# Block 1's recurrence: the sequential part of a chunk and the masked products of the next placed between the products of the levels

## What is computed

```python
def _rwkv7_time_mix(z, ...):
    ...
    def step(state, inp):
        r_t, d_t, k_t, v_t, kk_t, b_t = inp
        s_a = jnp.einsum('bhvk,bhk->bhv', state, -kk_t)
        state = state * d_t[:, :, None, :] + s_a[..., None] * b_t[:, :, None, :] + v_t[..., None] * k_t[:, :, None, :]
        return state, jnp.einsum('bhvk,bhk->bhv', state, r_t)
    ...
    _, y = lax.scan(step, jnp.zeros((B, H, N, N), f32), xs)
    ...group norm over each head, bonus, gate
```

## Time and profile before

| | us |
|---|---|
| median of 3 runs | 3438.39 (3433.8 to 3445.05) |
| the profiled execution's own time | 3441.6 |
| its span | 3439.8 |
| mean granted clock over the span | 0.93 |
| PE busy | 3057.2 (89%) |
| DVE busy | 1426.8 (41%) |
| ACT busy | 1173.5 (34%) |
| POOL busy | 1203.9 (35%) |

### The profile page before, as it was taken

One profiled execution on the slowest core, in us unless ns is written; L12 is line 12 of the kernel. 1 busy time (PEld: TensorE's weight loads), 2 busy tenths in 40 slices (PEclk: granted clock), 3 DMA queues, 4 the chain that ended last, 5 costly groups with the idle time before them and its releaser, 6 DMA issues.

```text
span 3439.8 us, 40156 instructions
## 1 busy us (share of the span) xinstructions
PE 3057.2 (89%) x15600; PEld 2375.6 (69%) x15600; DVE 1426.8 (41%) x2055; ACT 1173.5 (34%) x1681; POOL 1203.9 (35%) x558
## 2 busy tenths in 40 slices
PE   7989766778999999798999999978768787899998
PEld 5856535766888886576788887746557566688886
DVE  3017535325521274403356443251377352556442
ACT  3243241224322243543442224333433522542222
POOL 3413421103444444332645443403103221445442
PEclk9989877879999999899999999979889889999999
DMA  3312110004233332223532222302102111532222
GB/s 123 98 61 71 50 34 1 2 2 153 92 98 98 93 134 75 92 80 119 167 100 98 92 98 92 110 22 79 46 28 74 55 53 38 193 112 93 98 93 85
DMA packets 80667, 284.07 MB, mean 83 GB/s; under 512 B 8968, under 2 KB 9096, under 8 KB 79744
## 3 DMA queue, kind: packets, MB, share of 16 engines
q1 hardware_dynamic: 66240, 236.36, 21.3%
q10 hardware_dynamic: 13296, 41.97, 3.3%
q0 software_dynamic: 976, 3.56, 0.3%
HBM read 260.86 MB, written 20.99 MB: 82 GB/s over the span
## 4 chain that ended last, share of the span: by engine, by line
PE 55%; issue 19%; DVE 11%; POOL 9%; ACT 5%; DMA 1%; POOLq 0%; SPq 0%; ACTq 0%; DVEq 0%
PE bank L317 14%; PE bank L319 14%; PE bank L318 14%; POOL slab_r L2558 8%; PE bank L530 2%; PE bank L508 1%; PE bank L424 1%; PE bank L580 1%; DVE work L2355 1%; DVE work L2040 1%; DVE small L2038 1%; PE bank L434 1%; PE bank L759 1%; PE bank L818 0%; DVE work L2027 0%
## 5 line engine op out<-in xcount | busy, mean ns | idle before, releaser
L2558 POOL TENSOR_TENSOR slab_r<-slab,slab_high 128x1024 fp32r<-128x1024 f32 x442 | 1094.4, 2478 | 1764.5 <-ACT slab_high L1031 1764.1
L317 PE MATMUL bank<-xh,slab_high 128*128 128x512 f32 x2256 | 908.2, 403 | 35.6 <-POOL slab_r L2558 31.1
L319 PE MATMUL bank<-xh,slab_r 128*128 128x512 f32 x2256 | 889.8, 394 | 0.0
L318 PE MATMUL bank<-x_raw_r,slab_high 128*128 128x512 f32 x2064 | 815.8, 395 | 0.0
L1031 ACT CAST slab_high<-slab 128x1024 fp32r<-128x1024 f32 x442 | 462.3, 1047 | 450.8 <-DMA slab<-in_w_down 215.3
L318 PE MATMUL bank<-work_r,slab_high 128*128 128x512 f32 x1376 | 547.0, 398 | 0.0
L317 PEld LDWEIGHTS bank<-xh,slab_high 128*128 128x128 f32 x2256 | 431.5, 191 | 148.6 <-POOL slab_r L2558 34.9
L317 PE MATMUL bank<-work_r,slab_high 128*128 128x512 f32 x1184 | 474.0, 400 | 48.6 <-DVE work_r L1782 24.9
L319 PEld LDWEIGHTS bank<-xh,slab_r 128*128 128x128 f32 x2256 | 430.8, 191 | 93.8
L319 PE MATMUL bank<-work_r,slab_r 128*128 128x512 f32 x1184 | 475.5, 402 | 0.0
L318 PEld LDWEIGHTS bank<-x_raw_r,slab_high 128*128 128x128 f32 x2064 | 395.5, 192 | 80.6 <-issue 1.7
(11 more groups left out here) (434 smaller groups left out, 2942.3 us busy)
## 6 DMA issues: line engine op xcount, KB each, us to landing
slab<-in_w_down SPq DMA_DIRECT2D x88, 512.0 KB, 3.3
slab<-in_w_up SPq DMA_DIRECT2D x64, 512.0 KB, 3.2
slab<-in_w_gates SPq DMA_DIRECT2D x56, 512.0 KB, 3.4
slab<-in_w_merge SPq DMA_DIRECT2D x48, 512.0 KB, 3.7
slab<-in_w_gu SPq DMA_DIRECT2D x44, 512.0 KB, 3.5
slab<-in_w_in_a SPq DMA_DIRECT2D x32, 512.0 KB, 3.6
gates<-staging ACTq DMA_DIRECT2D x56, 256.0 KB, 2.2
slab<-in_w_out SPq DMA_DIRECT2D x24, 512.0 KB, 3.3
```

The lines of the kernel that those rows point to most:

```text
L317: first = pe.matmul(bank[b][:, :], wh, mh, start=start, stop=False)
L318: pe.matmul(bank[b][:, :], wh, ml, start=False, stop=False)
L319: end = pe.matmul(bank[b][:, :], wl, mh, start=False, stop=stop)
L2558: pool.tensor_tensor(slab_low[:, slot, :], slab[:, slot, :], plain(slab_high[:, slot, :]), ALU.subtract).then_inc(S("slab_split"), 1)
```

## The change

The recurrence of chunk n and the inverse of chunk n+1 are interleaved in the lists of PE, ACT and DVE.

- PE's `merge_levels` takes a function `beside(lv)` that is called between the first and the second product of each level. For chunks 1 to 3 it issues the preceding chunk's right side in level 1, the inverse times the right side in level 2, the outputs in level 3 and the new state in level 4. For chunks 0 to 2 it issues the next chunk's masked products, heads 0 to 2 in level 4, 3 to 5 in level 5, 6 and 7 in level 6. In level 6 it also issues the chunk's own transposes. Only chunk 0's masked products, and chunk 3's right side, inverse product and outputs, stand alone.
- The pieces set beside the levels use banks 0 to 3 (the masked products all four, where they used two) and have semaphores of their own (`act_beside`, `dve_beside`). The start matrix is turned into banks 6 and 7 instead of 4 and 5.
- Two chunks are alive at once, so masked products, whole inverse, the two level matrices and the packed blocks have two sets of tiles. The second set lies in the memory of `xh` and of `x_raw`, which hold nothing needed at that time (tile numbers from `NW` on).
- DVE masks the heads in levels 4 to 6 behind the level's update, and starts the next inverse behind level 6. ACT copies the transposed tiles behind level 6, then packs the next chunk's blocks, then copies the diagonal blocks of the whole inverse.
- In block 3 the helpers are called in their new, divided form.

The diff, cut to its core:

```diff
+        PRODUCTS, WHOLE, LEVEL_X, PACKED = (40, NW + DC), (50, NW), (48, NW + 2), (53, NW + 4)
+        HEADS_IN = {4: (0, 1, 2), 5: (3, 4, 5), 6: (6, 7)}
...
+            def turn_start(x, first):
...
+            def merge_levels(x, tt, am, off, waits, beside):
...
                         products.append(last[4 + hf])
-                    early_gates(fill)
+                    beside(lv)
                     for hf in halves:
                         pe.wait_ge(*products[hf])
...
+            def whole_inverse(waits, fresh):
...
+            def masked_products(ch, heads):
-                for src, b in ((8, 4), (12, 5), (24, 6)):
-                    tokens = turn([(W(src + c)[:, cs], c * P) for c in range(4)], b, "act")
-                for h in range(8):
+                for h in heads:
+                    r, b = half[h % 2], h % 4
                     if last[b]:
...
+                        .then_inc(psum_for["dve_beside"], hand(b, "dve_beside"))
+                if 7 in heads:
+                    mark(f"products{ch}")
+            def turn_operands(ch):
+                cs = slice(ch * P, (ch + 1) * P)
+                turned_at[ch] = [turn([(W(src + c)[:, cs], c * P) for c in range(4)], b, "act_beside")
+                                 for src, b in ((8, 0), (12, 1), (24, 2))]
+            def right_side(ch):
...
                 if ch:
                     pe.wait_ge(S("state_ready"), n.next(S("state_ready")))
+                for w in turned_at[ch]:
+                    pe.wait_ge(*w)
                 for par in range(2):
-                    if last[4 + par]:
-                        pe.wait_ge(*last[4 + par])
-                at = lambda c, par: bank[4 + par][:, c * HD:(c + 1) * HD]
+                    if last[par]:
+                        pe.wait_ge(*last[par])
...
+                    ins = pe.matmul(at(c, par), W(PRODUCTS[ch % 2] + h)[:, 2 * P:3 * P], W(30)[:, h * HD:(h + 1) * HD],
                                     start=(ch == 0 and c == 0), stop=(c == 3))
                     if c == 3:
-                        ins.then_inc(psum_for["dve"], hand(4 + par, "dve"))
-                early_gates(IN_SEQUENCE)
+                        ins.then_inc(psum_for["dve_beside"], hand(par, "dve_beside"))
+            def inverse_times(ch):
+                whole_inverse(inverse_at[ch], ch < 2)
                 for par in range(2):
-                    pe.wait_ge(*last[4 + par])
-                if last[6]:
-                    pe.wait_ge(*last[6])
+                    pe.wait_ge(*last[par])
+                if last[2]:
+                    pe.wait_ge(*last[2])
...
+                    ins = pe.matmul(bank[2][:, hs], W(WHOLE[ch % 2], 2)[:, h * P:(h + 1) * P], W(57)[:, hs],
                                     start=True, stop=True)
+                ins.then_inc(psum_for["act_beside"], hand(2, "act_beside"))
+            def outputs(ch):
+                at = lambda c, par: bank[par][half[par], c * P:(c + 1) * P]
+                pe.wait_ge(*last[2])
...
+                        ins.then_inc(psum_for["act_beside"], hand(par, "act_beside"))
+            def state(ch):
+                if last[3]:
+                    pe.wait_ge(*last[3])
+                for keys, values in ((28, 56), (29, 30)):
+                    for c, par in pairs:
+                        ins = pe.matmul(bank[3][half[par], c * HD:(c + 1) * HD], W(keys)[:, cols(c, par)],
+                                        W(values)[:, cols(c, par)], start=(keys == 28 and c == 0),
+                                        stop=(keys == 29 and c == 3))
+                ins.then_inc(psum_for["dve_beside"], hand(3, "dve_beside"))
+            masked_products(0, range(8))
+            start_at = turn_start(LEVEL_X[0], 6)
+            for ch in range(NT):
+                def beside(lv, ch=ch):
+                    if ch and lv <= 4:
+                        (right_side, inverse_times, outputs, state)[lv - 1](ch - 1)
+                    if ch < NT - 1 and lv in HEADS_IN:
+                        masked_products(ch + 1, HEADS_IN[lv])
+                    if lv == 6:
+                        turn_operands(ch)
+                inverse_at[ch] = merge_levels(LEVEL_X[ch % 2], 52, lambda lv: 54 + lv % 2,
+                                              lambda h, ch=ch: W(PRODUCTS[ch % 2] + h)[0:HD, HD:P], start_at, beside)
                 if ch < NT - 1:
-                    if last[7]:
-                        pe.wait_ge(*last[7])
-                    for keys, values in ((28, 56), (29, 30)):
-                        for c, par in pairs:
-                            ins = pe.matmul(bank[7][half[par], c * HD:(c + 1) * HD], W(keys)[:, cols(c, par)],
-                                            W(values)[:, cols(c, par)], start=(keys == 28 and c == 0),
-                                            stop=(keys == 29 and c == 3))
-                    ins.then_inc(psum_for["dve"], hand(7, "dve"))
-            pe.wait_ge(*y_token)
+                    start_at = turn_start(LEVEL_X[(ch + 1) % 2], 6)
+            for step in (right_side, inverse_times, outputs):
+                step(NT - 1)
+            y_tokens = [last[0], last[1]]
+            for w in y_tokens:
+                pe.wait_ge(*w)
...
+            def start_chunk(ch):
+                act.wait_ge(evac_by["dve_beside"], handed_at[f"products{ch}"]["dve_beside"])
+                pack_blocks([W3(PRODUCTS[ch % 2], 8)[:, :, 0:P]], PACKED[ch % 2], 8)
+                start_copies(LEVEL_X[ch % 2], 6)
+            def inverse_times():
+                act.wait_ge(for_beside, n.next(for_beside))
+                act.mul(W(56), bank[2][:, :], -1.0).then_inc(by_beside, n.up(by_beside))
...
+            start_chunk(0)
+            for ch in range(NT):
+                for lv in range(1, 7):
+                    level_copies(lv, 52)
+                    if ch and lv == 2:
+                        inverse_times()
+                    if ch and lv == 3:
+                        outputs(ch - 1)
+                for dst, b in ((28, 0), (29, 1), (30, 2)):
+                    act.wait_ge(for_beside, n.next(for_beside))
+                    act.copy(W(dst), bank[b][:, :]).then_inc(by_beside, n.up(by_beside))
+                if ch < NT - 1:
+                    start_chunk(ch + 1)
+                whole_copies(LEVEL_X[ch % 2] + 1, eight(WHOLE[ch % 2]))
+            inverse_times()
+            outputs(NT - 1)
+            act.wait_ge(by_beside, n.own(by_beside))
...
+            def masked_products(ch, heads):
+                for h in heads:
+                    dve.wait_ge(for_beside, n.next(for_beside))
+                    dve.tensor_tensor(W(PRODUCTS[ch % 2] + h).rearrange("p (a b) -> p a b", a=2), bank[h % 4][:,
                         :].rearrange("p (a b) -> p a b", a=2), two("strict"), ALU.mult)\
+                        .then_inc(by_beside, n.up(by_beside))
+            def start_chunk(ch):
+                dve.wait_ge(by_beside, n.own(by_beside))
+                inverse_start([W3(PRODUCTS[ch % 2], 8)[:, :, 0:P]], LEVEL_X[ch % 2] + 1, 8)
...
+            masked_products(0, range(8))
+            start_chunk(0)
+            for ch in range(NT):
+                for lv in range(1, 7):
+                    if lv < 6:
+                        level_update(LEVEL_X[ch % 2])
+                    if ch and lv == 1:
+                        right_side()
+                    if ch and lv == 4:
+                        state(ch - 1)
+                    if ch < NT - 1 and lv in HEADS_IN:
+                        masked_products(ch + 1, HEADS_IN[lv])
                 if ch < NT - 1:
+                    start_chunk(ch + 1)
+                dve.wait_ge(evac, n.own(evac))
+                coupling_block(eight(WHOLE[ch % 2]))
+            right_side()
```

198 lines of the change are left out of this document (93 added, 105 removed).

## The result

| | before | after |
|---|---|---|
| median of 4 runs each | 3437.9 us (3433.8 to 3445.1) | 3382.2 us (3379.0 to 3384.4) |
| ratio, 95% interval | 1 | 0.9835 [0.9817, 0.9853] |
| span of the profiled execution | 3439.8 us | 3380.2 us |
| recurrence of block 1 | 225.6 us | 167.1 us |

The change saves 55.7 us. It is 9 us less than the time of rival 1, 3391.

What follows compares the result with a forecast made beforehand. The prediction took the stage as one serial chain: 51.0 to chunk 1's level 1, chunks 1 to 3 45.3, 48.4, 38.3, last sequential part 14.5; 197.5 against 224.5 us, 27 less, 3411, range 3392 to 3431.

Steps and rivals of the forecast that it cites:

- rival 1: Whole stage: the clock stays high all through, 20 us more saved than forecast, 3391 us; chance 21%.
- Which clock?: Level 1 of chunks 1 to 3: low clock, 11.5 us (chunk 1 9.5); high clock from level 2 on.
- turning the start matrix: PE ahead of level 1: a thin 2.65 us with a wait of 0.67 behind it.
- the last sequential part: Chunk 3, standing alone: 14.5 us if part of it runs high, 16.3 before.
- The masked products: PE's own work 0.86 us a head on four banks, 8 x 0.86 = 6.9 a chunk.
- The prologue: Ahead of chunk 0's level 1: masked products without transposes, DVE done after 9.7 us; start 3.2; turning 2.7.
- The wait before L495: PE ahead of the start matrix: some 0.5 us of waiting where it waited 4.05.
- The outputs: Sequential part's outputs, inserted in level 3: 3 x 1.14 us at the high clock, 3.42.
- L718 and L732 at the high clock: Right side and inverse product, 64 columns: 2.0 us taken at the high clock, bounds 1.83 to 3.67.
- rival 4: Inserted pieces: each waits after all, about 1.2 us, eating the 8.4 us gain; 3438 us, chance 7%.
- Three masked heads in DVE's queue: Levels 4 and 5: DVE masks three heads in 1.95 us between two updates, so the update is not late.
- Rival 3: Levels: the clock stays low through them, a chunk 74.5 us against 56.8, 3483 us; chance 6%.

Runs made afterwards that it cites:

- seq_only: Changed kernel with the next chunk's masked products alone behind level 6, the sequential part still between the products of levels 1 to 4; 3404.6 us.
- idle_one: Changed kernel with one extra DVE multiplication of 128x512 ahead of the inverse's start in chunks 1 to 3; 3397.5 us.
- products_only: Changed kernel with the sequential part alone behind level 6 of its own chunk, masked products and transposes still among levels 4 to 6; 3386.7 us.
- behind: Changed kernel with the inserted work of levels 1 to 5 behind each level's second product instead of between the two; 3373.5 us.
- idle_start: Changed kernel with five extra DVE multiplications of 128x512 ahead of the inverse's start in chunks 1 to 3; 3419.7 us.
- four_banks: Kernel before with masked products going to banks 0 to 3 in turn instead of banks 4 and 5; 3431.8 us.

## Why the prediction was right and wrong

**Which clock?** This is the step that failed: "After the 0.5 us wait, a thin 2.65 us and its wait of 0.67 I expect the clock to fall", which put level 1 of chunks 1 to 3 at the low clock. The wait was 1.00, twice what was foretold, and the clock still did not fall. Level 1 took 5.1, 6.1 and 6.1 us instead of 9.5, 11.5 and 11.5, 15 us in all, and turning the start matrix 1.8 instead of 2.65, 2.5 more. The mechanism exists: seq_only and idle_one show the predicted level 1 line by line. The fault was to carry the fall behind 0.76 us in chunk 0, which came in the lone sequential part, over to a place with dense levels around it. The length of a wait alone does not decide: in the changed kernel itself the clock fell behind 0.82 us before L732 in the lone part, and held over 1.00 before L495. Which of the work before the wait and the work behind it matters, no run shows. The forecast was near an edge, between 1.00 and 1.60 us at this place, and the prediction had no row that placed it. Rival 1 deserved at least the forecast's chance, but it was not right as it stood: of the 20 us that it gave the clock 18 came, and the last sequential part was still low for half of its time (0.75).

**Size of the terms.** Taken from L2201's release, the stage took 31.5 us less than foretold. Clock and start matrix are 17.7 of them; of the other 14:
- The masked products. 0.86 a head was half of a pair's 1.91 less 0.18 of waiting, and it is the price of a head by itself. Neighbouring heads overlap in the two halves of the rows, and with two banks DVE's release had kept them apart. The eight heads of a chunk took 4.9 us instead of 6.9, three times: 5.9 us.
- The prologue. From L2201's release to level 1 of chunk 0 it took 12.0 us, 4.6 less than foretold: the heads again (2.8), the start matrix turned at the high clock (0.9), and L2033 (1.0), which took 0.69 in chunk 0 too and not the 1.8 foretold. DVE began it just ahead of POOL's mask (last section).
- The wait before L495, 1.00 for 0.5, cost 1.5 us more than foretold. The outputs (2.9 for 3.42 in chunks 2 and 3) and the last sequential part, at 13.7 for 14.5, make up 2.3; the last 2.5 us lie mostly in steps of 0.07, by which a group of matmuls begins ahead of its predecessor's end.

**What held.** L718 and L732 at the high clock: 2.00 foretold, 2.00 measured. The inserted steps wait for nothing, so rival 4 is out. Three masked heads in DVE's queue delay no update: the wait ahead of L529 stays at 0.72. The stage is one chain: 58.5 us less there, 59.6 in the span. Rival 3 needed half of a chunk's work low; in chunks 1 to 3 nothing was but the last sequential part.

**The rule against it.** The prediction weighed the Trainium skill (TensorE: Matmul & The Clock Gate, Part 1: The HAM clock gate), by which activity releases the clock and idleness brings it back, and set it aside because the sequential part ran at 0.50 with PE nearly always busy. The runs side with the rule on the levels (1.61 us of idleness lowers the clock, filling it restores it); they do not make the row wrong, since in products_only too L741 and L744 run low, one right behind the other.

## What to carry to other kernels

When a change moves work, ask which clock each piece will meet, and give the case "high all through" its own weight where every idle stretch shrinks to about 1 us. Test it cheaply with matmuls into an unread bank at the waits: in the stage half of this gain was to be had that way. In a serial chain put independent work where the next step waits for another engine, behind the level's last product, and let neighbouring 64-row matmuls use different halves of the rows.

## What the runs showed of the hardware

- At one place the clock's fall hangs on half a microsecond: 1.00 us of idleness before L495 left it at 2.4 GHz in three chunks of the changed kernel and three of behind, 1.60 brought 1.2 GHz in two of two (idle_one), and a fall cost about 5 us. Behind 6.5 us (idle_start) it once stayed low for 30 us. At another place, before L732 in the lone sequential part, 0.82 us was enough.
- The same instructions of block 0's attention, far ahead of the change, ran at either clock: in the profiles of four_banks and products_only at 1.00, in those of the other kernels without an edit there at 0.50. Busy time in 250 to 260 us, first of the kernel before, then of products_only:

```profile
250.00:260.00 10.00, 10.00 (x18) 4.16 (x17) 5.57 (x10) 4.14 (x8) 0.00 (x0) 0.50 0.00 0
```

```profile
250.00:260.00 10.00, 9.11 (x27) 3.93 (x27) 8.22 (x14) 5.40 (x10) 0.14 (x1) 1.00 0.00 0
```

  The stage under study then begins at 532 to 538 us or at 525 to 527. One kernel's runs fall into groups that fit this: those of four_banks are three at 3423.4 to 3423.8 and seven at 3431.2 to 3435.0, those of products_only 3381.9, 3382.4, 3391.0 and 3395.0, and the profiled ones (3423.4 and 3382.4) are among the short. So with an equal beginning products_only is about 11 us slower than the changed kernel, as the stages say, and not 4.4, as the medians say.
- DVE's subtraction took 0.69 us where it began 20 ns ahead of POOL's mask (544.33 and 544.35, after) and 1.79 where it began 10 ns behind the earlier trace rows.
